# Transposing the norm's first tiles ahead of a product's last unit, another unit order, and 32-wide blocks gathered by ScalarE

## What is computed

```python
# layer 0: h = rms_norm(x); q,k,v,z = h @ w_in; causal conv + silu; gated delta rule; @ w_out
a_strict = where(strict, beta * (k @ k.T) * decay, 0.0)          # 64-token chunks, 8 heads
sol = triangular_solve(a_strict, rhs, lower=True, unit_diagonal=True)
...
x = x + rms_norm(mix, post_mix_norm[layer])                      # "Mix" in the kernel
f = swiglu(rms_norm(x, pre_ffn_norm[layer]), w_ffn_in, w_ffn_out)
x = x + rms_norm(f, post_ffn_norm[layer])
# layer 1: k, v, forget gate from rms_norm(x, kv_norm) @ w_kv; q from another norm; softmax attention; swiglu
# third block: rms_norm(h) @ w_in_2 ... indexed and chunk-causal attention, gates, h + mixed @ w_out_2
```

## Time and profile before

| | us |
|---|---|
| median of 3 runs | 1896.92 |
| the runs | 1896.92, 1893.54, 1982.76 |
| the profiled execution, device time | 1895.08 |
| its span | 1893.3 |
| PE busy in it | 1782.8 |
| DVE, ACT, POOL busy | 680.8, 632.0, 691.1 |

### The profile page before, as it was taken

How to read it: one execution, slowest core, us unless ns; L and a number is a source line. 1 busy time by engine, 2 the same in 40 slices (tenths; PEclk the granted TensorE clock), 3 DMA queues, 4 the chain that set the end, 5 groups by cost and what they waited for, 6 DMA issues and landing times. The chain is left out here.

```text
span 1893.3 us, 24077 instructions
## 1 busy us (share of the span) xinstructions
PE 1782.8 (94%) x9646; PEld 1505.9 (80%) x9646; DVE 680.8 (36%) x1094; ACT 632.0 (33%) x939; POOL 691.1 (37%) x522
## 2 busy tenths in 40 slices
PE   5999899889999999998999999999999988989999
PEld 5777689688888887886899788888887886768777
DVE  3469326230100012332356220100114169988441
ACT  3633324232222224323334422222225222245540
POOL 2524133244544555341400434544554355620002
PEclk9999799999999999998999999999999999999989
DMA  4111112122222222221300122223221322210001
GB/s 178 68 67 67 46 67 77 69 76 102 89 102 108 89 103 86 101 98 38 112 1 1 67 70 109 89 93 128 89 94 68 124 103 89 89 45 23 1 1 45
DMA packets 22467, 145.40 MB, mean 77 GB/s; under 512 B 2640, under 2 KB 3280, under 8 KB 6384
## 3 DMA queue, kind: packets, MB, share of 16 engines
q1 hardware_dynamic: 22384, 144.22, 21.5%
HBM read 142.05 MB, written 2.10 MB: 76 GB/s over the span
## 5 line engine op out<-in xcount | busy, mean ns | idle before, releaser
L2233 POOL TENSOR_TENSOR wlo<-wraw,whi 128x512 fp32r<-128x512 f32 (+2 forms) x500 | 672.7, 1377 | 1149.6 <-ACT whi L132 1149.6
L132 ACT ACTIVATE whi<-wraw 128x2048 fp32r<-128x2048 f32 (+2 forms) x125 | 235.4, 1883 | 329.8 <-PE PS L318 194.5
L405 PE MATMUL PS<-hT_hi,whi 128*128 128x512 f32 x704 | 273.9, 389 | 0.0
L406 PE MATMUL PS<-hT_lo,whi 128*128 128x512 f32 x704 | 273.9, 389 | 0.0
L407 PE MATMUL PS<-hT_hi,wlo 128*128 128x512 f32 x704 | 273.9, 389 | 0.0
L1469 DVE TENSOR_TENSOR act_sb<-sil,PS 128x512 f32 x44 | 30.3, 688 | 428.6 <-ACT sil L1445 428.6
L407 PEld LDWEIGHTS PS<-hT_hi,wlo 128*128 128x128 f32 x704 | 132.1, 188 | 27.7
L405 PEld LDWEIGHTS PS<-hT_hi,whi 128*128 128x128 f32 x704 | 132.2, 188 | 27.4
L406 PEld LDWEIGHTS PS<-hT_lo,whi 128*128 128x128 f32 x704 | 132.2, 188 | 27.0
L1445 ACT ACTIVATE sil<-PS 128x512 f32<-128x512 f32 x44 | 26.4, 599 | 355.4 <-PE PS L407 335.5
L436 PE MATMUL PS<-whi,hT_hi 128*128 128x512 f32 (+2 forms) x320 | 122.2, 382 | 11.1 <-ACT vb L1893 3.5
(11 more groups left out here) (361 smaller groups left out, 3194.4 us busy)
## 6 DMA issues: line engine op xcount, KB each, us to landing
wraw<-wpack SPq DMA_DIRECT2D x125, 1024.0 KB, 4.8
gain<-gains SPq DMA_DIRECT2D x10, 512.0 KB, 6.1
x_sb<-x SPq DMA_DIRECT2D x8, 512.0 KB, 7.3
out<-x_sb SPq DMA_DIRECT2D x4, 512.0 KB, 2.6
csb<-consts SPq DMA_DIRECT2D x1, 768.0 KB, 6.7
vlat<-vecs SPq DMA_DIRECT2D x1, 320.0 KB, 3.0
vh<-vecs SPq DMA_DIRECT2D x1, 96.0 KB, 4.2
small<-vecs SPq DMA_DIRECT2D x1, 80.0 KB, 11.8
```

What stands on the lines that cost most here:

```text
L132: act.activation(whi[q % 2][:, w], wraw[q % 2][:, w], ACT.Copy).then_inc(w_hi, 1)
L405: nc.tensor.matmul(o, whi[q][w], hT_hi[:, k, :], start=(k == 0), stop=False)
L406: nc.tensor.matmul(o, whi[q][w], hT_lo[:, k, :], start=False, stop=False)
L2233: p.tensor_tensor(wlo[q][:, a:b], wraw[q][:, a:b], whi[q][:, a:b].bitcast(F32), ALU.subtract).then_inc(w_lo, 1)
```

## The change

It has four parts. Line numbers below are those of the kernel before, unless a row of the changed kernel is shown.

1. `pe_last` runs the units in the order (0,0) (0,1) (1,0) (1,1) (0,2) (0,3) (1,2), then transposes tiles 0 and 1 of the coming norm, then runs (1,3). Before, the order was (0,0) (0,1) (1,0) (0,2) (1,1) (0,3) (1,2) (1,3), and the transposes came behind it.
2. Three heads (both feed-forwards and the key projection) start with the products and transpose tiles 2 and 3 inside the second slot; the third block's head does so too. The weights' low parts are waited for by pieces there. The heads of the first norm and of the query projection stay as they were.
3. `CHAIN` is M0 M1 N0 N1 R T0 T1 M2 M3 S N2 N3 T2 T3, and ACT takes one root of a constant ahead of it.
4. ACT gathers the diagonal blocks into W for both halves (`act_blocks`, 4 copies of 32x512 each), DVE transposes them in one instruction of 128x1024; behind the elimination DVE writes W and blk in two instructions, `pe_pairs` waits for these two, and ACT makes the other five copies (`act_blocks_out`, 32x1024 each), for which `pe_pairs_out` waits.

```diff
+                if early:
+                    T.tile_done(t, 1)
+                    feat_tile(n, 0, piece=True)
+                    feat_tile(n + 1, 0, halves=(0,), piece=True)
+                    T.pe_tile(2)
+                    T.pe_tile(3)
+                    feat_tile(n + 1, 0, halves=(1,))
+                    T.tile_done(t, 3)
+                    for m in range(2):
+                        feat_tile(n + m, 2)
+                    return
...
-                for m, t in ((0, 0), (0, 1), (1, 0), (0, 2), (1, 1), (0, 3), (1, 2), (1, 3)):
+                for m, t in ((0, 0), (0, 1), (1, 0), (1, 1), (0, 2), (0, 3), (1, 2)):
                     slot(m, [t])
+                if turn:
+                    turn.pe_tile(0)
+                    turn.pe_tile(1)
+                slot(1, [3])
...
-        CHAIN = ["M0", "N0", "M1", "R", "N1", "S", "T0", "T1", "M2", "M3", "N2", "N3", "T2", "T3"]
+        CHAIN = ["M0", "M1", "N0", "N1", "R", "T0", "T1", "M2", "M3", "S", "N2", "N3", "T2", "T3"]
...
+            nc.scalar.activation(warm[:, mix.n0 // TT:mix.n0 // TT + 1], epsb[:, :], ACT.Sqrt).then_inc(sem("warm"), 1)
...
+        def act_blocks(hf):
+            a, hv = nc.scalar, lambda b: AT[quad(b), :, quad(b)].rearrange("p (c h) i -> p c h i", c=TT)[:, :, hs(hf), :]
+            a.wait_ge(sem("AT"), 4 * hf + 4)
+            for b in range(4):
+                a.activation(W[quad(b), :, 0:32].rearrange("p (c h) i -> p c h i", c=TT)[:, :, hs(hf), :], hv(b),
+                             ACT.Copy).then_inc(sem("diag"), 1)
+        def act_blocks_out():
+            a = nc.scalar
+            a.wait_ge(sem("inv"), 2)
+            a.activation(W[quad(1), :, 32:64], W[quad(1), :, 0:32], ACT.Copy).then_inc(sem("inv_out"), 1)
+            for b in (1, 3, 0, 2):
+                a.activation(AT[quad(b), :, quad(b)], blk[quad(b), :, :], ACT.Copy).then_inc(sem("inv_out"), 1)
...
-            for b in range(4):
-                v.transpose(blk[quad(b), :, :].rearrange("p k i -> p i k"),
-                            AT[quad(b), :, quad(b)].rearrange("p n i -> p i n")).then_inc(dve_step, 1)
+            v.wait_ge(sem("diag"), 8)
+            v.transpose(blk.rearrange("p k i -> p i k"), W[:, :, 0:32].rearrange("p n i -> p i n")).then_inc(dve_step, 1)
...
-            v.transpose(W[quad(1), :, 32:64].rearrange("p n j -> p j n"), by_row[quad(1), :, :]).then_inc(sem("inv"), 1)
-            for b in (1, 3, 0, 2):
-                v.transpose(AT[quad(b), :, quad(b)].rearrange("p n i -> p i n"), X3[quad(b), :, :]).then_inc(sem("inv"), 1)
+            v.transpose(blk.rearrange("p n i -> p i n"), X3).then_inc(sem("inv"), 1)
...
-            t.wait_ge(sem("inv"), 6)
+            t.wait_ge(sem("inv"), 2)
...
+            t.wait_ge(sem("inv_out"), 5)
...
+            N2.T.tile_done(nc.tensor, 1)
+            for c in range(TT):
+                if c > 1:
                     N2.T.tile_done(nc.tensor, c)
+                for m in range(2):
+                    if c == 1 and m == 1:
+                        N2.T.pe_tile(2)
+                        N2.T.pe_tile(3)
+                    tok_slot(n + m, 4 * m, 4, COLS[STEPS[0]], 0, m == 0, m == 1, tiles=[c], piece=True)
```

More of the change, by code:

```diff
@@ L212, in dve, with pe_head @@
                         self.T.dve(t - 1)
-            def pe_head(self, n, before=None, between=None, tile=None):
+            def pe_head(self, n, before=None, between=None, tile=None, early=False):
                 t, T = nc.tensor, self.T
+                if early:
[9 more added lines that the diff above has]
+                    return
                 for c in range(0, TT, 2):
@@ L323, in pe_slot, with pe_last @@
                         last.then_inc(w_used, 1)
-            def pe_last(self, slot):
-                for m, t in ((0, 0), (0, 1), (1, 0), (0, 2), (1, 1), (0, 3), (1, 2), (1, 3)):
+            def pe_last(self, slot, turn=None):
+                for m, t in ((0, 0), (0, 1), (1, 0), (1, 1), (0, 2), (0, 3), (1, 2)):
                     slot(m, [t])
+                if turn:
+                    turn.pe_tile(0)
+                    turn.pe_tile(1)
+                slot(1, [3])
             def act_sq(self, t):
@@ L359, in x_ready @@
                 eng.wait_ge(sem("mix_x"), self.n0 + t + 1)
-        CHAIN = ["M0", "N0", "M1", "R", "N1", "S", "T0", "T1", "M2", "M3", "N2", "N3", "T2", "T3"]
+        CHAIN = ["M0", "M1", "N0", "N1", "R", "T0", "T1", "M2", "M3", "S", "N2", "N3", "T2", "T3"]
+        warm = stat(4)
         def act_chain(mix, norm, split):
+            nc.scalar.activation(warm[:, mix.n0 // TT:mix.n0 // TT + 1], epsb[:, :], ACT.Sqrt).then_inc(sem("warm"), 1)
             for kind, *t in CHAIN:
@@ L408, in feat_slot, with feat_tile @@
             last.then_inc(w_used, 1)
-        def feat_tile(n, t, row=None):
+        def feat_tile(n, t, row=None, halves=range(2), piece=False):
             q, ts = n % 2, slice(t * P, (t + 2) * P)
-            for h in range(2):
+            for h in halves:
                 for k in range(KT):
@@ L416, in feat_tile @@
                     o = PS[:, 2 * q + h, ts]
+                    if piece and h == 0 and k % 2 == 0:
+                        piece_ready(nc.tensor, n, k // 2)
                     nc.tensor.matmul(o, whi[q][w], hT_hi[:, k, ts], start=(k == 0), stop=False)
@@ L772, in dve_blocks_in @@
             v.memset(XB, 0.0).then_inc(dve_step, 1)
[L773 to L776 removed]
+            v.wait_ge(sem("diag"), 8)
+            v.transpose(blk.rearrange("p k i -> p i k"), W[:, :, 0:32].rearrange("p n i -> p i n")).then_inc(dve_step, 1)
+            stepped(2)
             v.memset(XB[:, 0:1024:33], 1.0).then_inc(dve_step, 1)
@@ L1216, in pe_gdn @@
             gout_slot(1, [3])
-            GOUT.pe_last(lambda m, tiles: gout_slot(2 + m, tiles))
+            GOUT.pe_last(lambda m, tiles: gout_slot(2 + m, tiles), NF0.T)
         def act_gdn():
@@ L1246, in act_gdn @@
             act_silu(6)
+            act_blocks(0)
             act_tap(8)
@@ L1259, in act_gdn @@
             act_silu(10)
+            act_blocks(1)
             for n in range(6, 10):
@@ L1269, in act_gdn @@
             act_pairs(1)
+            act_blocks_out()
             act_tap(21)
@@ L1389, in pe @@
                 t = nc.tensor
-                self.norm.pe_head(self.b)
+                self.norm.pe_head(self.b, early=True)
                 def step(i):
@@ L1424, in pe @@
                 out(-1, NP - 3)
-                self.mix.pe_last(lambda m, tiles: out(NP - 2 + m, NP - 2 + m, 0, tiles, m == 1 and tiles[0] == 0))
+                self.mix.pe_last(lambda m, tiles: out(NP - 2 + m, NP - 2 + m, 0, tiles, m == 1 and tiles[0] == 0),
+                                 self.next.T)
             def hi_of(self, static, i=0):
@@ L1685, in pe_foxproj @@
             t = nc.tensor
-            NKV.pe_head(BASE["fk"])
+            NKV.pe_head(BASE["fk"], early=True)
             pe_heads("fk")
@@ L1693, in pe_foxproj @@
                 for m in range(2):
-                                        tok_slot(b + 2 * cb + m, 4 * m, 4, 512, 4 - 4 * cb, m == 0, m == 1, piece=True)
+                    tok_slot(b + 2 * cb + m, 4 * m, 4, 512, 4 - 4 * cb, m == 0, m == 1, piece=True)
             t.wait_ge(sem("fv"), 1)
@@ L1765, in pe_fox, with pe_rows @@
             FT_.pe()
-        def pe_rows(mix, stage, turn):
+        def pe_rows(mix, stage, turn, after=None):
             def slot(m, tiles):
@@ L1778, in pe_rows @@
             slot(1, range(TT))
-            mix.pe_last(lambda m, tiles: slot(2 + m, tiles))
+            mix.pe_last(lambda m, tiles: slot(2 + m, tiles), after)
         def act_rows(mix, stage, norm):
@@ L2191, in _ @@
             pe_fox()
-            pe_rows(FO, "fo", FT_)
+            pe_rows(FO, "fo", FT_, NF1.T)
             F1.pe()
```

7 lines of the change are left out of this document (removed).

## The result

The changed kernel took **1960.13 us** in the median of 4 executions (1959.17 to 1962.07), beside 1896.53 for the kernel before: a ratio of **1.034 [1.032, 1.036]**, slower. The forecast was 1869 with a range of 1859 to 1885, and "slower" had 0.02.

A forecast was written before the change was run, and what follows sets the result against it. PE's work, clock pace and waits were taken to bound the kernel. From 1895.1 us, 11.3 (joint waits), 6.5 (joint clock) and 11.2 (solve) came off and 2.6 (N2) was added: 1868.7, said as 1869, range 1859 to 1885.

The forecast's parts named there:

- the change removes no PE work: Whole kernel: the same transposes, units and products run in another order, so only PE's waits and clock were counted.
- The likeliest case: Whole kernel: the forecast of 1869 us, with 1864 to 1874, given a chance of 0.60.
- all four rivals: Joints' waits stay, 1886 (0.17); ACT's wait misses PE, 1861 (0.12); late copies or clock, 1875 (0.09); slow strided copies (0.02).
- a term of 1.6 us: Joint to N2: a half-clock window behind a wait of 2.3 to 2.4 us, costing 1.6 us (nothing to 1.7).
- the 11.3 of the sum: Joints to NF0, NKV and NF1: PE's waits fall by 3.9 at NF0 and 3.7 at NKV and NF1, 11.3 us.
- the waits move rather than go: Joints: xn, hT_lo or low pieces come 1.5 to 2 us late, so each joint waits again; 1886 us, chance 0.17.
- the 6.3 of the prediction: Joint to NF0: split S starts at 385.3 us, with PE ready for the transposes at 379.04.
- four stretches of the kernel before as gone, 6.5 us: Half-clock windows: 1.6 us each at NF0, NKV and NF1's first wait, 1.7 behind NF1's second, all to go.
- a forecast of +2.6: Joint to N2: waits cost 1.0 us more and a half-clock window 1.6 more.
- 4.4 for E: Solve, before the elimination: ACT's first four block copies make the tap 4.4 us late, and PE waits as long.
- the 1.6 in the sum: Solve: low clock behind PE's 4.4 us wait costs 1.6 us (nothing to 3.5).
- clock longer low behind the 4.4: Solve: copies behind the elimination are late or the clock stays low longer, so the solve gives 5; 1875 us, chance 0.09.

The follow-up runs named there:

- the burst: The changed kernel with ten extra matmuls of 128x512 between the attention's scores of unit 10 and transposes of unit 8: 1889.4, 1890.1, 1904.2 and 1910.2 us.
- thin products: The kernel before with eight extra matmuls of 64 columns behind the scores of each of the attention's first three units: 1904.7, 1968.2, 1980.9 and 1987.6 us.
- the second trace: The changed kernel run once more with nothing altered: 1880.8 us, the one profiled, and five executions of 1957.8 to 1964.9.
- The kernel with late copies: The changed kernel with four filler matmuls at the attention's entry and ACT's first four block copies moved behind the last decay: 1869.9 us, 0.988 of the kernel before.

## Why the prediction was wrong, point by point

**What failed.** The sum took each joint and the solve apart and counted everything between them as unchanged. That is the step that failed: "the change removes no PE work", so the rest keeps its time. The attention kept its work and its wait, and took 79 us more. The fall at its entry I had read in no view; the window row of the kernel before (926.00:933.00 at 0.51) was in the trace, beside a wait as short as those of the earlier trace rows, and I priced low clock only behind waits that the change moves. The likeliest case, all four rivals and the range share this. None had "the same wait, the same code, another length of the low clock". The Trainium skill, "TensorE: Matmul & The Clock Gate", section "What's actually happening", says that the gate is set by how busy the engine has lately been, and that its timing runs free of the kernel. The traces agree with both: the burst raised the clock, thin products kept it down, and in three traces of the changed kernel's code the fall lay at 2.00, 1.97 and 1.41 us of the entry. Busy can't mean there that PE is never idle, since at 0.50 it was without one idle moment for 160 us. I had set that section against a term of 1.6 us and passed over what it means for a long stretch of thin work.

Without the attention's 79.0 us the profiled execution would have been at 1883.1, and the second trace's took 1880.8: inside the range, but 12 to 14 us above the forecast. These are terms that I mis-sized.

**The joints' waits.** On hT_lo nothing is left, as forecast; what PE waits for is wlo. PE's waits of the changed kernel, 370 to 410 us:

```profile
PE PS L437 <- POOL wlo L2272: 2.2, 2, 1.2
```

The same row answers the earlier trace rows at NKV and stands at NF1. The gains are 5.2 - 2.2 = 3.0 and twice 5.0 - 2.2 = 2.8, together 8.6 for the 11.3 of the sum. The rival "the waits move rather than go" had the direction, at 2.7 us of its 11.3. S started 6.1 us behind the first transpose (380.04 and 373.98), the 6.3 of the prediction. What was off is the pace of the pieces:

```profile
382.01 6.97 POOL L2272 TENSOR_TENSOR wlo<-wraw,whi 128x512 fp32r<-128x512 f32 x4 [3.26 <-ACT whi L132]
```

```profile
383.80 1.85 DVE L190 SCALAR_TENSOR_TENSOR xn<-x_sb,small,gain 128x1024 f32<-128x1024 f32 x1
385.58 0.15 DVE L184 RECIPROCAL small<-small 128x1 f32<-128x1 f32 x1
385.77 2.10 DVE L190 SCALAR_TENSOR_TENSOR xn<-x_sb,small,gain 128x1024 f32<-128x1024 f32 x1
```

The first row is POOL's, the others DVE's. A piece took 1.74 us (6.97 over 4) and not the 1.37 of the earlier trace rows, and DVE's two xn took 1.85 and 2.10 where the one of the earlier trace rows took 1.29: the two engines slow each other when S's pieces run beside xn of tiles 2 and 3. The 1.37 was itself a mean over both cases, for in the kernel before the xn of tile 1 ran beside those eight pieces:

```profile
380.16 2.04 DVE L190 SCALAR_TENSOR_TENSOR xn<-x_sb,small,gain 128x1024 f32<-128x1024 f32 x1
```

All 14 traces together bear it out: the 220 xn with no piece beside them took 1.27 to 1.29 us, those wholly beside pieces 1.86 in the median and up to 2.10, while the 24 scaled sums in PSUM of the same size wholly beside pieces kept their 1.29. With S ahead of M3 the pieces ran at 1.27 us (5.08 over 4) and their start came 6.8 us behind the transposes instead of 8.0; that took the whole wait away.

**The half clock at the joints.** I counted four stretches of the kernel before as gone, 6.5 us. Two are left, at 388.8 and 1160.2:

```profile
388.80:392.20 3.40, 3.16 (x15) 3.16 (x16) 0.00 (x0) 0.60 (x1) 0.18 (x1) 0.50 0.58 176
1160.20:1163.60 3.40, 3.40 (x18) 3.40 (x17) 1.27 (x2) 1.55 (x3) 0.00 (x0) 0.50 0.82 284
1528.80:1532.20 3.40, 3.40 (x8) 2.65 (x9) 0.00 (x0) 0.00 (x0) 0.00 (x0) 0.50 1.01 400
```

So two waits of 1.0 and 1.2 us with 1.2 us of matmuls between them were followed by it at two joints, and not at NKV, which has the same two waits. That is 3.3 us of the gain lost. The third row is N2's stretch, which the sum had.

**N2.** Its waits for wlo: forecast 2.3 and three of 0.68, 4.4 in all; the row of PE's waits, 1510 to 1540 us, answers the earlier trace rows:

```profile
PE PS L456 <- POOL wlo L2272: 4.7, 4, 2.0
```

That was right. From the first transpose of tile 0 to that of tile 2 the kernel before took 16.1 us and the changed one 20.1, +4.0 for a forecast of +2.6.

**The solve.** The waits came as worked out. PE's waits of the changed kernel, 100 to 210 us:

```profile
PE PS L722 <- ACT E L745: 4.4, 1, 4.4
PE PS L785 <- DVE bv L794: 1.8, 2, 1.6
PE PS L543 <- issue: 1.2, 1, 1.2
PE PS L845 <- DVE blk L832: 0.6, 1, 0.6
```

4.4 for E was forecast as 4.4, bv as 1.3 (two waits of 0.2 and 1.6 here), blk as 1.1 (0.6 here). A copy of 32x512 on ACT took 0.63 us each, 0.59 assumed; the strided copies are not slow. The size was off by the clock:

```profile
105.50:115.70 10.20, 7.83 (x21) 5.87 (x22) 1.45 (x2) 3.77 (x6) 0.00 (x0) 0.50 0.01 2
...
192.00:200.00 8.00, 7.42 (x142) 6.40 (x142) 2.95 (x4) 5.34 (x7) 0.04 (x1) 0.64 0.42 133
200.00:206.00 6.00, 6.00 (x152) 5.21 (x154) 1.30 (x2) 3.68 (x4) 0.00 (x0) 0.91 0.01 3
```

Behind the 4.4 us the clock was low for 10.2 us, worth more than the 1.6 in the sum, and the stretches behind the elimination did not all go but partly moved. At the start of `pe_pairs` (198.84 before) PE was 5.9 us ahead, and 5.0 in the second trace, for 7.7 in the sum; at the joint to NF0 it was 7.8 and 9.0 for 11.2. The kernel with late copies shows the price of the 4.4 us with its clock: 1878.6 to 1869.9, 8.7 us in all, not 6.0, though on two chips whose medians of the kernel before differ by 2.0. The rival "clock longer low behind the 4.4" (1875) was right about this place.

**The whole.** In the second trace PE is 20.8 us ahead at the joint to N2; the forecast had 29.0 there. It then gives back 6.6 for a forecast of 2.6. Of these 4.0 are N2's; the other 2.6 lie behind it and weren't traced further.

## What to carry to other kernels

A clock that falls behind a wait costs what the work behind it makes of it: before taking a stretch as unchanged, look in the trace for every short wait at the door of a long run of small matmuls, and for a low clock behind it, even one that came back. If there is one, the kernel may have two times, and a change anywhere ahead of it may move the odds. Filler matmuls into the wait removed the question here for 3.4 us, of which 1.55 had been waited; put them in both kernels before the two are compared. Price a producer's pieces by what its neighbours do at that moment, not by the row of a quiet stretch.

## What the runs showed of the hardware that I had not expected

- A low clock held for 171 us while PE was never idle: 676 matmuls in 160 us at 0.50 against 709 in 87 us at 1.00. In another execution a burst of matmuls of 512 columns ended it within 2.5 us.
- One wait of 1.55 us decided 80 us, while the wait of 5.23 us that ended at 854 us, 58 us ahead of it, came with a low clock of only 6.8 us. In one of ten traces the short wait was followed by no low clock at all.
- Two waits of 1.0 and 1.2 us close together were followed by a low clock of 3.4 us at two of three joints.
- DVE's xn and POOL's pieces beside each other took 1.85 to 2.10 us and 1.74 us, alone 1.29 and 1.27.
